# Three weight products of a one-core kernel: the weight's high part runs over both halves of the input in one instruction

## The reference, cut to what matters

```
# layer 1 of the first block (only the 256 latent tokens are needed there)
xl  = layer_norm(ALPHA * xl + gt1_l * (o_l @ w_out), ln1_g[1], ln1_b[1])       # "dout", 1024 -> 1024
f_l = (silu(conv(h @ w_gate)) * (h @ w_up)) @ w_down                            # "down", 2816 -> 1024
xl  = layer_norm(ALPHA * xl + gt2_l * f_l, ln2_g[1], ln2_b[1])
# second block
h = h + concatenate([y_ssd, y_sc], -1) @ w_out[l]                               # "wout", 2048 -> 1024
```

## Time and profile before

| | us |
|---|---|
| median of 3 executions (1573.57 to 1578.92) | 1575.02 |
| profiled execution, its own time | 1571.35 |
| its span in the trace | 1569.6 |
| TensorE busy | 1511.9 (96%) |
| VectorE busy | 846.8 (54%) |
| ScalarE busy | 734.9 (47%) |
| mean granted TensorE clock | 0.997 |

### The profile page before, as it was taken

The page is one execution under the profiler, slowest core; times in us unless marked ns, Lnnn a source line. Parts: engine busy times, 40 slices in busy tenths (PEclk is TensorE's granted clock), DMA queues, the critical chain, the costliest instruction groups (busy, mean ns, idle before and its releaser), DMA issues.

```text
span 1569.6 us, 25484 instructions
## 1 busy us (share of the span) xinstructions
PE 1511.9 (96%) x10510; PEld 1172.4 (75%) x10510; DVE 846.8 (54%) x1492; ACT 734.9 (47%) x1151; POOL 1.4 (0%) x6
## 2 busy tenths in 40 slices
PE   7999989999999999999999999999999999999987
PEld 5645668777787778879978899998998899534443
DVE  2547666744333444665387875767478884312213
ACT  3545562633322333363365663545555653655544
POOL 0000000000000000000000000000000000000000
PEclk9999999999999999999999999999999999999999
DMA  9412633344433443433202355533444345999996
GB/s 388 182 41 81 213 111 107 135 161 161 164 118 134 161 163 109 144 136 133 84 25 82 135 182 181 199 123 140 171 154 143 135 176 202 425 425 425 427 427 243
DMA packets 36376, 288.27 MB, mean 184 GB/s; under 512 B 4112, under 2 KB 4240, under 8 KB 11552
## 3 DMA queue, kind: packets, MB, share of 16 engines
q1 hardware_dynamic: 35936, 285.93, 48.1%
q0 software_dynamic: 176, 0.59, 0.1%
q10 hardware_dynamic: 144, 0.06, 0.0%
HBM read 285.51 MB, written 1.05 MB: 183 GB/s over the span
## 4 chain that ended last, share of the span: by engine, by line
PE 81%; DVE 7%; DMA 5%; ACT 4%; issue 2%; DVEq 0%; SPq 0%; ACTq 0%
PE ps L557 17%; PE ps L558 16%; PE ps L559 16%; PE ps L3035 6%; DMA deep<-wts 5%; PE ps L608 2%; DVE WL L542 2%; PE ps L1490 1%; PE ps L1588 1%; ACT WH L532 1%; PE ps L1559 1%; PE ps L2911 1%; PE ps L1660 1%; PE ps L1659 1%; PE ps L1658 1%
## 5 line engine op out<-in xcount | busy, mean ns | idle before, releaser
L542 DVE TENSOR_TENSOR WL<-ring,WH 128x2048 fp32r<-128x2048 f32 (+2 forms) x134 | 281.2, 2103 | 139.7 <-ACT WH L532 139.5
L557 PE MATMUL ps<-HH,WH 128*128 128x512 f32 (+2 forms) x944 | 325.1, 344 | 4.5 <-DVE WL L542 3.6
L558 PE MATMUL ps<-HL,WH 128*128 128x512 f32 (+2 forms) x944 | 320.1, 339 | 0.0
L559 PE MATMUL ps<-HH,WL 128*128 128x512 f32 (+2 forms) x944 | 320.0, 339 | 0.0
L532 ACT ACTIVATE WH<-ring 128x2048 fp32r<-128x2048 f32 (+2 forms) x134 | 236.2, 1765 | 170.2 <-PE ps L559 93.6
L557 PEld LDWEIGHTS ps<-HH,WH 128*128 128x128 f32 (+1 forms) x944 | 178.8, 189 | 44.2 <-issue 19.3
L559 PEld LDWEIGHTS ps<-HH,WL 128*128 128x128 f32 (+1 forms) x944 | 178.9, 189 | 20.2
L558 PEld LDWEIGHTS ps<-HL,WH 128*128 128x128 f32 (+1 forms) x944 | 179.0, 190 | 18.3
L557 PE MATMUL ps<-UHL,WH 128*128 128x256 f32 (+3 forms) x416 | 121.9, 293 | 4.0 <-DVE UHL L2702 2.1
L3035 PE MATMUL ps<-deep,arena 128*32 128x512 f32 (+1 forms) x808 | 114.6, 593 | 7.2 <-ACT other_b L3021 4.1
L557 PE MATMUL ps<-parts,WH 128*128 128x512 f32 (+1 forms) x352 | 119.1, 338 | 0.4 <-DVE WL L542 0.4
(11 more groups left out here) (428 smaller groups left out, 2494.2 us busy)
## 6 DMA issues: line engine op xcount, KB each, us to landing
ring<-wts SPq DMA_DIRECT2D x138, 1024.0 KB, 4.9
deep<-wts SPq DMA_DIRECT2D x39, 2048.0 KB, 18.3
ring<-wts SPq DMA_DIRECT2D x32, 704.0 KB, 4.1
under_x<-wts SPq DMA_DIRECT2D x6, 2048.0 KB, 21.8
arena<-wts SPq DMA_DIRECT2D x8, 1024.0 KB, 16.1
deep<-wts SPq DMA_DIRECT2D x4, 1024.0 KB, 27.0
ring<-wts SPq DMA_DIRECT2D x4, 672.0 KB, 13.7
X<-xin SPq DMA_DIRECT2D x4, 512.0 KB, 16.5
```

The lines of the kernel that those rows point to most:

```text
L542: e.tensor_tensor(lo, raw(i), hi.bitcast(F32), ALU.subtract).then_inc(*up("low", i))
L557: e.matmul(o, w[0][:, cols], x[0], start=k == 0, stop=False)
L558: e.matmul(o, w[0][:, cols], x[1], start=False, stop=False)
L559: return e.matmul(o, w[1][:, cols], x[0], start=False, stop=k == nk - 1)
```

## The change

In the three places with 256 tokens the first two products of a group become one of 512 columns: the high weight runs over the input's high and low parts, which lie at a fixed distance in one tensor and are named by a two-step access pattern. Columns 0 to 255 of the bank take high by high, columns 256 to 511 take high by low. The third product (low weight by high input) still has 256 columns and adds into columns 0 to 255. In the last group of a tile the 256-column product goes first. VectorE then adds two halves of the bank to the residual instead of one, the second add waiting for the first by a semaphore. `HH` and `HL` become one tensor `HHL` with the same layout.

```
+        def mm3_wide(e, b, w, cols, x, k, nk):
+            first = lambda stop: e.matmul(ps[:, b, :], w[0][:, cols], x, start=k == 0, stop=stop)
+            second = lambda stop: e.matmul(ps[:, b, 0:256], w[1][:, cols], x[:, 0, :], start=False, stop=stop)
+            if k == nk - 1:
+                second(False)
+                return first(True)
+            first(False)
+            return second(False)
...
         def pe_out_pair(e, key, src, arrive, n, tag):
...
-            two_tiles(e, c, weights(e, c), [ps[:, b, 0:n] for b in bs], src, key + (0,), True, (arrive,))
+            w = weights(e, c)
+            for k in range(8):
+                e.wait_ge(*at(arrive, k))
+                for m in range(2):
+                    t = mm3_wide(e, bs[m], w, slice(256 * k + 128 * m, 256 * k + 128 * m + 128),
+                                 src[:, :, 256 * k:256 * k + 256], k, 8)
...
         def pe_out(e, key, nk, src, arrive, n, mt_per, l, tag, mean=True, pair=False):
...
+                        if n == 256:
+                            t = mm3_wide(e, b, w, cols, src[:, :, 256 * k:256 * k + 256], k, nk)
+                        else:
+                            t = mm3(e, ps[:, b, 0:n], w, cols, at_k(src, k, slice(0, n)), k, nk)
...
         def dve_out(e, key, n, mt_per, l, gt, tag, nxt):
...
+                    if n == 256:
+                        e.scalar_tensor_tensor(out=X[:, j, 0:256], in0=B("out", key, j)[:, 256:512],
+                                               scalar=modv[l][:, gt + j, 0:1], in1=X[:, j, 0:256], op0=ALU.mult,
+                                               op1=ALU.add).then_inc(*up("y.low", tag, j))
+                        e.wait_ge(*at("y.low", tag, j))
...
         def pe_wout_tiles(e, half, i, order):
...
-                t = mm3(e, ps[:, banks.of["wout", half, 2 * i + m], 0:NL], w,
-                        slice(256 * k + 128 * m, 256 * k + 128 * m + 128), at_k(YCP if half else YSP, k), k, 8)
+                t = mm3_wide(e, banks.of["wout", half, 2 * i + m], w, slice(256 * k + 128 * m, 256 * k + 128 * m + 128),
+                             YCX[:, :, k, :] if half else YPX[:, :, k, LATENT], k, 8)
...
         def dve_wout(e):
...
+                        e.tensor_tensor(R[:, j, LATENT], R[:, j, LATENT], B("wout", half, j)[:, NL:2 * NL],
+                                        ALU.add).then_inc(*up("mixed.part", half, j))
+                        e.wait_ge(*at("mixed.part", half, j))
                         e.tensor_tensor(R[:, j, LATENT], R[:, j, LATENT], B("wout", half, j)[:, 0:NL],
                                         ALU.add).then_inc(*up("mixed", half, j))
```

More of the change, by code:

```diff
@@ L413, in build @@
         WH, WL = (ctx.enter_context(nc.sbuf_tensor(n, [128, SPLITS * SLOT], F32R)) for n in ("WH", "WL"))
-        HH, HL = (ctx.enter_context(nc.sbuf_tensor(n, [128, 16 * NT], F32R)) for n in ("HH", "HL"))
+        HHL = ctx.enter_context(nc.sbuf_tensor("HHL", [128, 32 * NT], F32R))
+        HH, HL = HHL[:, 0:16 * NT], HHL[:, 16 * NT:32 * NT]
         deep_size = (SLOTS + 2 * SPLITS) * SLOT + 32 * NT
@@ L559, in mm3, with both_of @@
             return e.matmul(o, w[1][:, cols], x[0], start=False, stop=k == nk - 1)
+        def both_of(t):
+            return t.rearrange("p (s c) -> p s c", s=2)
+        def mm3_wide(e, b, w, cols, x, k, nk):
[6 more added lines that the diff above has]
+            return second(False)
         def two_tiles(e, n, w, o, x, name, by_k, arrive=None):
@@ L884, in pe_out_pair @@
             bs = [bank(e, "out", key, m) for m in range(2)]
-            two_tiles(e, c, weights(e, c), [ps[:, b, 0:n] for b in bs], src, key + (0,), True, (arrive,))
+            w = weights(e, c)
[4 more added lines that the diff above has]
+                                 src[:, :, 256 * k:256 * k + 256], k, 8)
+                    if k == 7:
+                        t.then_inc(*(up("used", c) if m else up("tile", *key, 0)))
             for m in range(2):
@@ L902, in pe_out @@
                             e.wait_ge(*at(*arrive(k)))
-                        t = mm3(e, ps[:, b, 0:n], w, slice(width * k + 128 * m, width * k + 128 * m + 128),
-                                at_k(src, k, slice(0, n)), k, nk)
+                        cols = slice(width * k + 128 * m, width * k + 128 * m + 128)
+                        if n == 256:
+                            t = mm3_wide(e, b, w, cols, src[:, :, 256 * k:256 * k + 256], k, nk)
+                        else:
+                            t = mm3(e, ps[:, b, 0:n], w, cols, at_k(src, k, slice(0, n)), k, nk)
                     t.then_inc(*(up("used", c) if m == mt_per - 1 else up("tile", *key, j)))
@@ L1006, in pe_ffn @@
                     pe_mod_end(e)
-                pe_out(e, ("down", l, half), HALF, ffn_parts(n), lambda k: ("part_low", l, HALF * half + k), n, 1, l, F_.tag,
-                       half == 1)
+                pe_out(e, ("down", l, half), HALF, ffn_parts(n) if l == 0 else both_of(PARTS),
+                       lambda k: ("part_low", l, HALF * half + k), n, 1, l, F_.tag, half == 1)
         def through(l, f):
@@ L1953, in build @@
         YSP = tuple(t[:, :, LATENT] for t in YP)
+        YPX, YCX = (t.rearrange("p (s a b) -> p s a b", s=2, a=8) for t in (UHL, YHL))
         top[0] = 0
@@ L3411, in tensor_program @@
             pe_diff(e)
-            pe_out(e, ("dout",), 8, OD, "od_low", 256, 2, 1, "n10", pair=True)
+            pe_out(e, ("dout",), 8, both_of(HHL), "od_low", 256, 2, 1, "n10", pair=True)
             pe_norm(e, N10, (), index["gu", 1, 0])
```

## The result

The changed kernel takes 1582.9 us (median of 15 executions, 1580.75 to 1587.35), the kernel before 1573.57 us on the same chip (median of 15). The ratio is 1.0057, 95% interval 1.0046 to 1.0068: slower by 9.0 us, 7 to 11. I had forecast 1577.6 us (+2.6 on the 1575.02 known then), no change that can be told, and a range up to 1582.0. The time lies above that range.

What follows compares the result with a forecast made beforehand. TensorE was taken to bound the kernel, with 81% of the chain of waits. Terms dout +1.6, down −1.1 and +0.4, wout +1.5, clock +0.2 gave +2.6 us on 1575.02: 1577.6 us, range 1573.0 to 1582.0.

Steps and rivals of the forecast that it cites:

- The clock (+0.2 forecast): In `wout`, the half-clock stretch behind TensorE's wait before block 7 may vanish (−1.35 us) or double (+1.35); taken as +0.2.
- rival (b): Longer TensorE waits, in `dout` and `wout`, bring half clock again, +1.35 us each; with two +5.3, 1580.3 us; chance 0.08.
- The adds (0.52 and 0.46): VectorE's additional add costs 0.52 us more for a tile of `dout` or `down`, 0.46 us in `wout`.
- forecast 1.6: `dout` gets 1.6 us longer: −0.42 from TensorE's first four tiles, then additional adds of 0.52, 1.04 and 0.52.
- forecast 4.6: In `wout`, TensorE's wait ahead of the one before block 7 becomes about 4.6 us.
- forecast 2.16: In `wout`, block 7's low part comes 2.16 us later: adds +2.76, TensorE's gain −0.37, absorbed in a VectorE wait −0.23.
- The saving of a group (0.013): In all three places, a group of products takes 0.347 us instead of 0.360, saving one product's fixed 0.013 us.
- `down`'s first half: TensorE is busy without a gap, additional adds stay covered, and 88 groups save 0.013 us each: −1.1 us.
- the 251 groups that counted: Groups whose saving reaches the sum: 32 of `dout`, 88 and about 50 of `down`, 28 + 53 of `wout`.
- down's second half (+0.4): −0.1 us up to tile 5's add, then tile 6's additional add +0.52 before ScalarE's square of tile 7: +0.4 us.
- After `wout`: Expert loads wait for the last `wout` product and then fill DMA to the end, so the end moves +1.47 us.
- the +2.4 of the forecast: The prediction's terms over `dout`, `down` and `wout` without the clock term: +2.4 us.

Runs made afterwards that it cites:

- the 95 executions above: Unchanged kernel before, measured beside the follow-up kernels, sorted by mean granted clock: from 1572.5 us at 0.997 and 0.998 to 1579.9 us at 0.990 to 0.993.
- the lowest class: Executions of the unchanged kernel before with a mean granted clock of 0.990 to 0.993: 12 executions, mean 1579.9 us.
- the 20 products: Kernel before plus 20 products without a reader in five of TensorE's waits, some longer than the wait: ratio 1.0011 to the kernel before, +1.7 us.
- the 15: Kernel before plus 15 products without a reader, no longer than TensorE's waits, no wide product: ratio 0.9976 to the kernel before, median 1570.82 us.

## Why the prediction was wrong, by its own steps

**The clock (+0.2 forecast): the step that failed.** I asked about the clock only where the kernel before already fell to half, in `wout`, and let gain and loss there nearly cancel. In the profiled execution after, the lower level lasted twice as long there (nearly 7 us instead of 3.4), but part of that fell into the wait. Behind the last low part six groups take 3.93 us (1314.75 to 1318.68) instead of some 2.1, a loss of 1.8 us; the fifteen products before took 3.29 (1305.25 to 1308.54) instead of 1.8, a loss of 1.5. So this place cost +0.3, near the +0.2 of the forecast. What I had at nothing were two more stretches, behind `dout` and `down`, 2.4 and 2.5 us. That is rival (b), which I gave 0.08 and priced at 1.35 us for each. Its price was about half of what came: I took it from a stretch of dense products, while in the layer norms VectorE stood waiting for the spreads. The argument against it was that the wait in `dout` (0.96 us) had left the clock alone. It did so after too, at 1.63 us; the clock fell behind the chain of short waits that follows. The mean clock of the executions says much the same: 0.9915 against 0.9957 (the 95 executions above; those of the comparison itself have no clock on record), 0.0042 of 1575 us, 6.6 us as an estimate.

**The adds (0.52 and 0.46): right**, 0.51 and 0.45, and so were their places. `dout` became 1.8 us longer (forecast 1.6), with TensorE's wait before the last chunk at 1.63 (forecast 1.7). In `wout` the wait before block 6 was 4.43 (forecast 4.6), and the low part of block 7 came 2.4 us later (forecast 2.16).

**The saving of a group (0.013): mis-sized.** 0.0075 on the mean in `down`; with wide and narrow kept apart it is 0.011. `down`'s first half gained 0.7 instead of 1.1. In `wout` it was 0.012 in half 1 (a pass of 16 groups took 6.46 us instead of 6.65) and 0.0035 in half 0 (a tile 3.47 instead of 3.50), where the groups before were quicker than 0.360 too. Taking `down`'s figure for the 251 groups that counted, 251 × 0.0055 = 1.4 us are missing, an estimate.

**down's second half (+0.4)** became +0.7, by the path that I had described: tile 6's first add started 4.1 us later (1074.80), its second one brought 0.5, and ScalarE's square of tile 7 came 4.6 later. The smaller saving of a group accounts for the other 0.3 (an estimate, some 50 groups × 0.0055). **After `wout`** the end moved with the last product, as forecast, and by 2 us more: between the last tile of `wout` (+9.6) and VectorE's last pair of steps (+11.55). DMA isn't full to the end, as I had written, but to about 1550 us. The last load landed 11.5 us later (ScalarE's wait for it ended at 1564.71 instead of 1553.20), so these 2 us arose while the loads ran, at 416 GB/s from 1329.6 to 1561.5 against 419 from 1320 to 1550. No experiment aimed at it, and its cause stays open; the comparison is of one execution each.

**The sum.** Forecast +2.6; with the mis-sized saving +4.0; with 6.6 − 0.2 for the clock +10.4, against 9.0 measured (7 to 11). For the two profiled executions the clock's places are 2.4 + 2.5 + 0.3 = 5.2, which gives +9.0; with the 2 us behind `wout` it is +11.0 of 11.5. The other way round, the 15 executions after took 1583.9 us on the mean, and those of before in the lowest class 1579.9. Of these 4.0 us, 1.1 are the clock again (0.9915 against 0.9922 within the class). So about 2.9 us are left at an equal clock, between the +2.4 of the forecast and the +3.8 with the saving corrected.

## What to carry to other kernels

An instruction that is added beside TensorE can cost its own time, and then what the longer wait does to TensorE's clock in the next stage of short steps that wait for one another. Ask that question at every place where TensorE has short waits and small products, not only where the profile at hand shows half clock, and compare that profile's mean clock with those of other executions first. Where the waits can't be shortened, a few products without a reader, shorter than the wait, gave 3.8 us here, where the change lost 9. Where some were longer than the wait, they cost what the clock gave back: at a mean clock of 0.999 the kernel before takes 1574.6 us with the 20 products (3 executions) and 1570.8 with the 15 (7 executions, not measured side by side).

## What the runs showed of the hardware that was not expected

- The granted clock fell to half behind several short waits in a row (1.49, 0.17 and 0.60 us, with 16 products of 64 columns between them), though not behind a single wait of 1.63 us in front of dense products (1.00 from 866 to 874 us). The mean clock of the kernel before went from 0.990 to 0.998 over 95 executions, and its time from 1585.2 to 1570.5 us, though its one trace shows no such stretch in the layer norms.
- A 512-column product with its moving operand in two pieces costs no more than one in one piece that a run can tell: 0.229 us in a run of eleven against 0.227 in the earlier trace rows, and 0.353 for a group in `dout` either way. The same pair of products at a granted clock of 1.00 took 0.354 us in most of `down`, 0.346 in half 1 of `wout`, and 0.349 where the wide and the narrow ones were kept apart.
